# Gathered down and up rows taken turn by turn, in four row places each, with the side pieces at half and at the end of a group

## What is computed

```
scores = q @ keys                     # top 16 x top 16 per head, 8 heads -> 128 experts per token
idx, gates = top experts, softmax of their scores
a   = sum_d h[token, d] * peer_down[idx[token, e], d]      # one dot product per token and expert
out = sum_e gates[e] * gelu(a[e]) * peer_up[idx[token, e], :]
```

## Time and profile before

| | |
|---|---|
| median of 3 runs | 4367.61 us (4365.7 to 4381.82) |
| the profiled execution, its own time | 4396.53 us |
| its span (first to last instruction) | 4394.7 us |
| busy: PE, DVE, POOL, ACT | 79%, 52%, 34%, 22% |
| the six gathers | from 432 us to 3215 us of the span, with 243 us of other work between c01 and x10 |

### The profile page before, as it was taken

One profiled execution on the slowest core, in us unless ns is written; L12 is line 12 of the kernel. 1 busy time (PEld: TensorE's weight loads), 2 busy tenths in 40 slices (PEclk: granted clock), 3 DMA queues, 4 the chain that ended last, 5 costly groups with the idle time before them and its releaser, 6 DMA issues.

```text
span 4394.7 us, 43630 instructions
## 1 busy us (share of the span) xinstructions
PE 3492.7 (79%) x14172; PEld 2260.8 (51%) x14172; DVE 2304.4 (52%) x4861; ACT 984.6 (22%) x1936; POOL 1505.2 (34%) x1746
## 2 busy tenths in 40 slices
PE   6998477899976677888788466666679869999799
PEld 2576133465542233345366222222269859797687
DVE  2215864444477763543334877344445666564364
ACT  2301112111111111211121111111133443334333
POOL 0000555555465666565400566666610000000000
PEclk8999788999987888999899788888889989999799
DMA  6574888899898999999723899999955415454244
GB/s 269 200 264 179 292 298 333 324 356 382 320 342 315 344 354 354 352 378 367 264 73 115 303 356 347 338 338 351 346 192 183 149 48 179 166 190 167 83 169 153
DMA packets 273572, 1157.22 MB, mean 263 GB/s; under 512 B 30848, under 2 KB 31616, under 8 KB 234496
## 3 DMA queue, kind: packets, MB, share of 16 engines
q0 software_dynamic: 221184, 805.40, 49.7%
q1 hardware_dynamic: 52224, 349.75, 21.6%
HBM read 1153.99 MB, written 1.05 MB: 263 GB/s over the span
## 4 chain that ended last, share of the span: by engine, by line
PE 54%; issue 14%; DVE 12%; DMA 11%; POOL 7%; ACT 1%; POOLq 0%; SPq 0%; DVEq 0%; another core or an unknown queue 0%; ACTq 0%
PE ps L889 17%; POOL rows L2156 7%; DMA rows<-in_peer_up,iup 7%; PE ps L938 5%; PE ps L940 5%; PE ps L939 5%; PE ps L814 5%; DMA rows<-in_peer_down,idown 4%; DVE rows L1731 4%; PE ps L648 4%; PE ps L859 3%; PE ps L837 2%; PE ps L1043 1%; PE ps L603 1%; PE ps L791 1%
## 5 line engine op out<-in xcount | busy, mean ns | idle before, releaser
L889 PE MATMUL ps<-rows,diag 128*128 128x512 f32 x3072 | 1480.0, 643 | 661.7 <-DMA rows<-in_peer_up,iup 651.3
L889 PEld LDWEIGHTS ps<-rows,diag 128*128 128x128 f32 x3072 | 629.2, 208 | 1493.8 <-issue 1069.0
L1731 DVE CUSTOM_DVE_ANT_0 rows<-rows,ps 128x1024 f32<-128x1024 f32 x768 | 920.5, 1219 | 651.5 <-DMA rows<-in_peer_down,idown 612.1
L2156 POOL DMA_INDIRECT rows<-in_peer_down,idown x768 | 730.4, 951 | 665.8 <-PE ps L889 376.9
L2156 POOL DMA_INDIRECT rows<-in_peer_up,iup x768 | 722.7, 941 | 355.4 <-issue 181.3
L1323 ACT ACTIVATE diag<-ident,act 128x128 f32<-128x128 f32 x768 | 281.5, 397 | 979.3 <-PE ps L889 515.0
L938 PE MATMUL ps<-hT_hi,w_hi 128*128 128x256 f32 x1600 | 451.8, 282 | 16.9 <-DVE hT_lo L1832 16.9
L940 PE MATMUL ps<-hT_lo,w_hi 128*128 128x256 f32 x1600 | 452.4, 283 | 0.0
L939 PE MATMUL ps<-hT_hi,w_lo 128*128 128x256 f32 x1600 | 451.4, 282 | 0.0
L2219 POOL TENSOR_TENSOR ss<-nwt,minus_half 128x2 f32<-128x2 f32 x13 | 9.0, 692 | 1174.8 <-DVE nwt L1529 1174.8
L1819 DVE TENSOR_TENSOR w_lo<-wring,w_hi 128x2048 fp32r<-128x2048 f32 x120 | 274.9, 2292 | 147.3 <-ACT w_hi L1382 145.5
(11 more groups left out here) (298 smaller groups left out, 3731.8 us busy)
## 6 DMA issues: line engine op xcount, KB each, us to landing
wring<-in_wgu SPq DMA_DIRECT2D x66, 1024.0 KB, 4.8
wring<-in_wdn SPq DMA_DIRECT2D x33, 1024.0 KB, 4.8
wring<-in_wG SPq DMA_DIRECT2D x29, 1024.0 KB
rows<-in_wmod SPq DMA_DIRECT2D x27, 1024.0 KB, 8.4
wring<-in_wpq SPq DMA_DIRECT2D x24, 1024.0 KB
rows<-in_wgu SPq DMA_DIRECT2D x22, 1024.0 KB, 4.7
wring<-in_wmod SPq DMA_DIRECT2D x21, 1024.0 KB
rows<-in_peer_down,idown POOLq DMA_INDIRECT x768
```

The costliest lines, as they stand in the source:

```text
L889: ins = pe.matmul(ps[:, UPB + half, :], diag[:, j % DIAGS, :], rows[:, j, half * 512:(half + 1) * 512], start=(first and j == 0), stop=(la ...
L1731: dve.tensor_tensor_reduce(out=rows[:, j, :], in0=rows[:, j, :], in1=h_ps, scale=1.0, scalar=0.0, op0=ALU.mult, op1=ALU.add, accum_out=a8[ ...
L2156: pool.indirect_dma_start(out=rows[:, j, :], out_offset=None, in_=table, in_offset=bass.IndirectOffsetOnAxis(ap=offs[:, j:j + 1], axis=0)) ...
```

## The change

Row places 0 to 3 are for down rows, 4 to 7 for up rows. POOL issues one down row of group n, one up row of group n-1, the next down row of n, and so on; each waits for the row four before it of its own kind. Each engine's list a now stands behind the fourth row of the group and b behind the eighth. ACT's program isn't changed. In group 0 POOL issues only down rows, and after group 15 only up rows.

```diff
 PE, gather:
-                def up(g, first=False, last=False):
-                    for j in range(GROUP):
-                        pe.wait_ge(row_in[j], 16 * (32 * G + 1) + 16 * pos_)
+                def up(g, js, first=False, last=False):
+                    for j in js:
+                        s = HALF + j % HALF
+                        pe.wait_ge(row_in[s], 32 * g + 16 * (32 * G + j // HALF + 1))
...
+                def group(n, stages_a=(), stages_b=()):
+                    if not is_group(n, 0):
+                        up(n - 1, range(HALF), first=is_group(n, 1))
+                    run_stages(stages_a)
+                    if not is_group(n, 0):
+                        up(n - 1, range(HALF, GROUP))
+                    run_stages(stages_b)
-                run_stages(beside_a)
-                groups(pe, n0, n1, lambda n: is_group(n, 0) or up(n - 1, first=is_group(n, 1)))
-                run_stages(beside_b)
 DVE, gather:
                 def group(n, stages_a=(), stages_b=()):
-                    down(n, first)
+                    down(n, range(HALF), first)
                     run_stages(stages_a)
+                    down(n, range(HALF, GROUP), first)
+                    gelu(n)
                     act_of(n, first)
                     run_stages(stages_b)
 POOL, gather:
+                def down(g, par, j):
+                    if G or not isinstance(g, int) or 8 * g + j >= HALF:
+                        pool.wait_ge(down_done, 8 * g + (P * G + j + 1 - HALF))
+                    fetch(A["peer_down"], idown[par][:, j:j + 1], j % HALF)
+                def up(g, par, j):
+                    if G or not isinstance(g, int) or 8 * g + j >= HALF:
+                        pool.wait_ge(upp_done, 8 * g + (P * G + j + 1 - HALF))
+                    fetch(A["peer_up"], iup[par][:, j:j + 1], HALF + j % HALF)
+                def group(n, par, ahead=True):
+                    pool.wait_ge(idx_copied, 2 * n + (2 * GROUPS * G + 1))
+                    for j in range(GROUP):
+                        down(n, par, j)
+                        up(n - 1, 1 - par, j)
+                        if j == HALF and ahead:
+                            offsets(idown[1 - par], n + 1)
+                            offsets(iup[par], n)
```

More of the change, by code:

```diff
@@ L32 @@
 GROUPS = P // GROUP
+HALF = GROUP // 2
 SLOTS = 3
@@ L881, in gather @@
                 G = GATHER_NO[run, t]
-                def up(g, first=False, last=False):
-                    pos_ = 31 if last else 2 * g + 2
-                    for j in range(GROUP):
-                        pe.wait_ge(row_in[j], 16 * (32 * G + 1) + 16 * pos_)
+                def up(g, js, first=False, last=False):
+                    for j in js:
+                        s = HALF + j % HALF
+                        pe.wait_ge(row_in[s], 32 * g + 16 * (32 * G + j // HALF + 1))
                         pe.wait_ge(diag_ready, 8 * g + (P * G + j + 1))
                         for half in range(2):
-                            ins = pe.matmul(ps[:, UPB + half, :], diag[:, j % DIAGS, :], rows[:, j, half * 512:(half + 1) * 512],
+                            ins = pe.matmul(ps[:, UPB + half, :], diag[:, j % DIAGS, :], rows[:, s, half * 512:(half + 1) * 512],
                                             start=(first and j == 0), stop=(last and j == GROUP - 1), skip_group_check=True)
                         ins.then_inc(upp_done, 1)
+                def group(n, stages_a=(), stages_b=()):
[5 more added lines that the diff above has]
+                    run_stages(stages_b)
                 if n0 == 0 and run != "c0" and t == 0:
@@ L902, in gather @@
                     at_mark(pe, "fin", GATHERS[G - 1][0], GATHERS[G - 1][1] + 1)
-                groups(pe, n0, n1, lambda n: is_group(n, 0) or up(n - 1, first=is_group(n, 1)))
-                run_stages(beside_b)
+                if beside_a or beside_b:
+                    group(n0, beside_a, beside_b)
+                else:
+                    groups(pe, n0, n1, group)
                 if n1 == GROUPS:
-                    up(GROUPS - 1, last=True)
+                    up(GROUPS - 1, range(GROUP), last=True)
             def fin(run, t):
@@ L1723, in gather, with down, gelu @@
                 G = GATHER_NO[run, t]
-                def down(g, first=False):
-                    if first:
+                def down(g, js, first=False):
+                    if first and js[0] == 0:
                         dve.wait_ge(h_copied, 2 * G + 2)
-                    for j in range(GROUP):
-                        dve.wait_ge(row_in[j], (16 * (32 * G + 1)) if first else 32 * g + 16 * (32 * G))
-                        dve.tensor_tensor_reduce(out=rows[:, j, :], in0=rows[:, j, :], in1=h_ps, scale=1.0, scalar=0.0,
+                    for j in js:
+                        s = j % HALF
+                        dve.wait_ge(row_in[s], 32 * g + 16 * (32 * G + j // HALF + 1))
+                        dve.tensor_tensor_reduce(out=rows[:, s, :], in0=rows[:, s, :], in1=h_ps, scale=1.0, scalar=0.0,
                                                  op0=ALU.mult, op1=ALU.add, accum_out=a8[:, j:j + 1]).then_inc(down_done, 1)
+                def gelu(g):
                     base = 3 * GROUPS * G
@@ L2153, in gather, with fetch @@
                 at_mark(pool, "route", run, 2 * t + 1)
-                def fetch(table, offs, j):
+                def fetch(table, offs, s):
                     pool.sem_inc(slot_ok, 1)
-                    pool.indirect_dma_start(out=rows[:, j, :], out_offset=None, in_=table,
-                                            in_offset=bass.IndirectOffsetOnAxis(ap=offs[:, j:j + 1], axis=0)).then_inc(row_in[j], 16)
+                    pool.indirect_dma_start(out=rows[:, s, :], out_offset=None, in_=table,
+                                            in_offset=bass.IndirectOffsetOnAxis(ap=offs, axis=0)).then_inc(row_in[s], 16)
                 def offsets(dst, g):
@@ L2161, in offsets @@
                     pool.tensor_copy(dst[:, :], src).then_inc(idx_copied, 1)
-                def down(g, par, first=None, ahead=None):
-                    for j in range(GROUP):
[L2165 to L2187, removed]
@@ L2189, in gather @@
-                offsets(idown[0], 0)
[L2190 to L2197, removed]
+                def down(g, par, j):
+                    if G or not isinstance(g, int) or 8 * g + j >= HALF:
+                        pool.wait_ge(down_done, 8 * g + (P * G + j + 1 - HALF))
+                    fetch(A["peer_down"], idown[par][:, j:j + 1], j % HALF)
@@ L2199, in gather @@
+                offsets(idown[0], 0)
+                pool.wait_ge(idx_copied, 2 * GROUPS * G + 1)
+                for j in range(GROUP):
+                    down(0, 0, j)
+                    if j == HALF:
+                        offsets(idown[1], 1)
+                        offsets(iup[0], 0)
+                group(1, 1)
                 with pool.Fori(1, GROUPS // 4 - 1) as m:
-                    pair(m)
-                pair(GROUPS // 4 - 1, False)
+                    group(m * 2, 0)
+                    group(m * 2 + 1, 1)
@@ L2202, in gather @@
+                group(GROUPS // 2 - 2, 0)
+                group(GROUPS // 2 - 1, 1, False)
                 at_mark(pool, "route", run, 2 * t + 2)
                 offsets(idown[0], GROUPS // 2)
+                offsets(iup[1], GROUPS // 2 - 1)
                 with pool.Fori(GROUPS // 4, GROUPS // 2 - 1) as m:
[L2205 to L2208, removed]
@@ L2209, in gather @@
-                down(m * 2 + 1, 1, ahead=(iup[0], m * 2))
-                up(m * 2, 0, ahead=(iup[1], GROUPS - 1))
-                up(GROUPS - 1, 1, True)
+                    group(m * 2, 0)
+                    group(m * 2 + 1, 1)
+                group(GROUPS - 2, 0)
+                group(GROUPS - 1, 1, False)
+                offsets(iup[1], GROUPS - 1)
+                pool.wait_ge(idx_copied, 2 * GROUPS * (G + 1))
+                for j in range(GROUP):
+                    up(GROUPS - 1, 1, j)
```

## The result

| | before | changed |
|---|---|---|
| median | 4374.72 us (4365.70 to 4383.57) | 4421.40 us (4419.52 to 4428.50) |
| ratio to before, 95% interval | 1 | 1.0103 [1.0072, 1.0134] |
| span of the profiled execution | 4394.7 us | 4426.7 us |

The changed kernel is 47 us slower, 1.0%. The forecast said 4285.6 us and a gain of 82 us, and the measured time lies outside its range too. The first view to read is again the page: the engines, then the chain that ended last by engine and by line.

What follows compares the result with a forecast made beforehand. The order, not an engine or DMA, was taken to bound plain groups; other stretches had other bounds. Terms -50 + 15 + 1 - 22 + 6 - 5 + 0 - 31 + 4 = -82 us gave 4285.6 us, range 4228 to 4378.

Steps and rivals of the forecast that it cites:

- what bounds a plain group: Plain groups: the order, not DMA or an engine, bounds them; alternating gives 21.6 us a group, -50 us in all.
- DMA-bound: Rival: DMA engines already full in plain groups; plain and ranking gains vanish, costs of PE's pieces stay; 4378 us, chance 0.12.
- memory limit: Rival: rows alone sustain little more than 346 GB/s, so a plain group takes 23.4 us; 4344 us, chance 0.06.
- TensorE's clock: Rival: short gaps after every row lower PE's clock, a group takes 27.5 us; 4548 us, chance 0.06.
- the step on side pieces on PE of length S: A group with a PE side piece takes S + 16.2 us, if above 21.6; x01 +15 us, c01's groups 1 to 11 +1.
- costly-pieces rival: Rival: weights and rows collide after each return, 3 us for each of 13 long PE pieces; 4336 us, chance 0.14.
- the +18 that I gave: x01: eight groups with PE pieces of 14 to 16 us cost 2.3 us each, +18 us.
- group 8: x01: gains about 10 us, as norm runs beside four rows instead of PE waiting for norm and rows.
- V + 15.2 us: Group time with a DVE side piece of length V; 16 groups in c00 and x10 -22 us, long ranking pieces +6.
- cost at nothing: Lone PE rows and the chain from eighth down row to first diagonal, about 2 us, stay hidden: 0 us.
- -31 us for x00: Rest of x00: about 9 us sooner after a 16.9 us piece, -22 for six attention groups, 0 for two gates.
- gates of over 32 us: Sign of being wrong: x01's gate groups taking over 32 us, where about 30 us was expected.

Runs made afterwards that it cites:

- rows_first_again: The changed kernel, but in x01 alone DVE handles rows 5 to 8 of a group before its first list of side pieces; 4435.87 us, ratio to before 1.0139.
- x11_only: The kernel before, but gather x11, which has no side pieces, takes the new order; 4336.10 us, ratio to before 0.9915.

## Why the prediction was wrong

**Right: what bounds a plain group.** The order did. In turns POOL hardly waits, and 16 x 1.24 us plus 0.7 us of copies, loop and short waits make the 20.6 us measured. I had named 20.8 us as the low end and taken 21.6 us because of the DMA engines; they gave 406 GB/s over 247 us. With a busy share of 1.02 they may be close to their own limit; no run tells the two apart. The rivals DMA-bound, memory limit and TensorE's clock are out on this chip: the clock was granted 1.00 with a gap of 0.6 us after every row, where the Trainium skill (page TensorE: Matmul & The Clock Gate, section A second HAM failure mode) tells of a kernel whose clock swung with brief idles between groups of matmuls. The 358 GB/s for a core of the Trainium skill (page DMA: Bandwidth & Descriptors, section Where 436 GB/s comes from) is exceeded by 48 GB/s here. The 352 GB/s of the slower chip lie just under it; whether that limit is their cause isn't shown.

**Wrong: the step on side pieces on PE of length S.** I put S + 16.2 us. The first kind of gate, S = 14, measured 32.1 to 32.3 us, so S + 18.3. What failed is "the following three come every 2.5 us". The first up row after the return is issued at 1047.13 and used at 1051.62, S + 7.2 for the S + 7.5 forecast. The next three are used at 1055.61, 1058.67 and 1061.14, so 4.0, 3.1 and 2.5 us apart: POOL issues them every 2.5 us, but they take 6.0 to 6.6 us from issue to use, where I had 5.6 us for all, read from a single row of the old order. The chain of waits behind that gate (start, us, what) has 6.52 us of transfer for one up row:

```profile
1054.58 6.52 DMA rows<-in_peer_up,iup
...
1061.14 1.98 PE ps L890 x4
```

In c01 the term repeats: 32.5, 32.4 and 32.2 us for pieces of 14 us and 25.3 and 25.4 for 7 us, where I had 30.2 and 23.2. The costly-pieces rival had this size, at 3 us a piece, and was given 0.14. Its reason, that weights and rows collide, isn't shown and isn't needed: in the plain groups of x11, where no weights are loaded, a row takes 5.3 to 7.4 us from issue to landing, 7.2 in the median.

**Wrong: "pieces" were priced on one engine at a time.** The sum had no term for a DVE list that waits for PE's list with rows behind it. It costs 2 to 3 us in four of the six groups, every second gate and both `out` (rows_first_again), on top of the 2.1 us above. The parts of x01, before to after: the nine groups with gates or long pieces +46.5 us for the +18 that I gave; the first group +10.5 for +5; group 8 +1.3 for -10: PE no longer waits 4.90 us for norm, but it waits 9.4 us for rows instead of 4.71, as POOL stood 6.95 us while DVE was away with norm; the last five +2.4 for +2. This is 60.7 for 15, and the largest part of the miss.

**Wrong in size: ranking pieces, V + 15.2 us.** From the last down row of one group to that of the next, a short one measured 23.1 to 25.4 us for the 22.7 forecast, a long one 26.6 to 27.4 for 25.2. What was missing is again POOL's strict order: the four rows in hand cover 4 x 2.5 us only on paper, since POOL stops both kinds once one is full (its wait of up to 7.6 us for DVE), and the up rows behind the stop come late. In one such group of x10:

```profile
2615.70 0.94 POOL L2171 DMA_INDIRECT rows<-in_peer_down,idown  x1 [3.63 <-DVE a L1742]
2619.66 2.44 ACT L1333 ACTIVATE diag<-ident,act 128x128 f32<-128x128 f32 x8 [0.49 <-DVE act L1763]
2622.30 3.25 PE L890 MATMUL ps<-rows,diag 128*128 128x512 f32 x4 [2.76 <-DMA rows<-in_peer_up,iup]
```

PE waits 2.76 us for the up row that POOL issued right behind that stop, with its diagonal begun 2.6 us before. So my "cost at nothing" held: the chain from the eighth down row to the first diagonal takes 1.3 us, for the 2 us that I gave it. PE starts 3.7 to 4.4 us after the eighth down row in these groups and 2.7 us after it in x11, and in both it waits for the row. With halves it is mostly 2.6 us, and the short ones take 20.9 to 22.6 us.

**Wrong: -31 us for x00.** All of the -15.6 us measured was chance in the execution I read. Its ranking groups took 27.1 us there and 25 in another run of the same order (23.1 and 27.0 by turns), and x00 is the same length in both orders. I had noted that the execution lay 28.9 us above the median and then spread nothing of it over the gathers; 16 us sat in x00. Part by part against x11_only, whose x00 has the old order: the six groups with attention pieces gained 14.6 us for the 22 forecast; the two groups before them, where I had -9, lost 6.7 us; the first ranking groups, at nothing in the sum, lost 7.8 us, and the rest 0.6 us.

**The signs.** The prediction named gates of over 32 us as a sign of being wrong, and they took 32 to 35 us. Slower had 0.11, of the clock and of DMA-bound. What came true is a mix: DMA-bound's "costs of PE's pieces stay, gains vanish" without the DMA limit. Had I taken the costly pieces (+50), their upper bound S + 16.7 (+0.5 for some 15 pieces) and V + 16 (+0.8 for 21), the sum would have been -82 + 50 + 8 + 17 = -7 us; the missing wait, group 8, the late rows in ranking groups and x00 are what changed the sign.

## What to carry to other kernels

Before an order is made strict on the queue that feeds two consumers, count for each how long it is away without a break, and compare that with the rows in hand: with four places of a kind, pieces of 3.7 us cost little here (two of them in a group, 1 us) and pieces of 7 us and more stopped both kinds. Make long pieces short first (halved ranking pieces brought nothing clear of noise in the old order; in the new one c00 and x10 took 751 us with them and 813 without), and use the new order only in the stretches where it fits. For each list put between two halves of a loop, ask for which other engine's list it waits, and what stands behind it.

## What the runs showed of the hardware

- One core drew 406 GB/s by indirect row gathers of 524 KB for 247 us, with POOL issuing one every 1.24 us and a DMA busy share of 1.02.
- The time from issue to landing of such a row grew with what was under way: 4.5 us for the first after a stop in x01, 7.2 us in the median of x11's plain groups.
- Another chip, in one set of runs, gave the same program 352 GB/s in the same stretch, 13% less. The kernel with the new order was 2.9% slower there (4563.48 for 4435.87 us), the one before, which idles between bursts, 0.5%: the faster order also depends more on the rate of the rows.
- TensorE was granted 1.00 through rows of 1.98 us with gaps of 0.6 us; in the old order, with 8 us at rest per group, it had 0.85.
